# A two-block network kernel on one core: three steps on unsplit weights at the start, another spread of c, and more banks in the convolution stage

## The chip, the cores and the metric

The kernel runs on 1 core of one Trainium2 chip. The metric is device time in microseconds (us); lower is better. Engines are called by the profile's names: PE is TensorE, ACT is ScalarE, DVE is VectorE, POOL is GpSimd, SP is SyncE, whose queue issues all DMAs.

## The reference

Two transformer-like blocks run one after the other on a sequence of 256 tokens with 1024 features, all in float32. What matters here is the beginning of the first block:

```python
c_act = jax.nn.silu(c)
mod = (c_act @ w_ada[i] + b_ada[i]).reshape(bsz, N_MOD, D_MODEL)[:, :, None, :]
shift1, scale1, gate1 = mod[:, 0], mod[:, 1], mod[:, 2]
...
u = rms_norm(x, ln1[i]) * (1.0 + scale1) + shift1
proj = u @ w_in                                   # 1024 -> 13,344 columns
gl, cb, cc, cx, z, xbc, dt = jnp.split(proj, split_at, axis=-1)
...
xbc = jax.nn.silu(causal_depthwise_conv(xbc, ssm_conv_w) + ssm_conv_b)   # 4 taps
dt = jax.nn.softplus(dt + dt_bias)
a = -jnp.exp(a_log)
y = ssd_scan(xs * dt[..., None], dt * a, bs, cs)
```

The rest of both blocks (gates, scan, output projections, an MLP of 4096, two kinds of attention, an MLP of 2816) is large matrix products with the same weights-times-activations form; the change doesn't touch it.

## The kernel before, in words

All activations lie transposed, features on the 128 partitions and 256 tokens along the row. `plan()` cuts all weight matrices into about 141 steps of 1024 rows x 256 columns (1 MB each), `steps[n]`. A step gives two output groups (`nb` 0 and 1) of 128 columns each; group `i = 2*n + nb` is accumulated in one PSUM bank over eight k-tiles.

A product in full precision is made of three products on rounded operands: weights are split into `w_hi` (ACT, `split_hi`, a copy that rounds) and `w_lo` (DVE, `split_lo`, raw minus hi), activations into `uh` and `ul` (`lo_part`, POOL). PE then does hi*hi, hi*lo and lo*hi for each k-tile, 48 matrix products a step (L1160, `product_part`). In steps 4 to 17 (`TAILS`) DVE makes only the first five of eight k-tiles of `w_lo`, and POOL the other three (`split_tail`). The buffers `raw`, `w_hi` and `w_lo` have three slots each.

The first `NAT` = 2 steps are done otherwise: `first_part` multiplies the raw float32 weights by the unrounded activation `uf`, 16 slower products a step, so that nothing has to be split for them. Between these products, `keep_busy` issues idle products so that PE stays active.

The start goes like this. Eight tiles `ada_w` hold the columns of `w_ada` for shift and scale; for each, DVE multiplies it by the activated row c (`cact`, broadcast to all partitions by DMA) and sums along the row, once for scale and once for shift (`early_ada`, L1481), then makes `gain` (L1484). ACT squares x, PE sums the squares over the partitions (`x_sum`), and ACT makes the root (`x_root`, Ln and Exp). POOL multiplies x by the root into `uf`, ACT applies gain and shift twice, for `uh` (rounded) and `uf`, and POOL makes `ul`. PE's `first_part` waits for `uf`.

Steps 0 to 15 are the kind `xbc`, the convolution stage. For group i, ACT initialises `cv` from the bank (L931, the last tap with bias), DVE adds three taps from the bank (L1626, three linked instructions, the last of which frees the bank), and ACT does Silu into `xs` or `bct` (L983). Their banks rotate over `acc0` to `acc2`, and `cv` has two slots.

Woven into the stage are: `dt` (a thin product after step 3, transposed after group 10), its softplus on ACT (`log1p_exp_parts`) and DVE (`softplus`) at `SOFT_AT` = step 5, the cumulative sums at `CUM_AT` = step 8, and from slot 18 (`slot = 2*n + nb`) on sixteen transposes of `xs` (`x_transpose`) in banks M3 and M4 in turn, each of which DVE multiplies by dt into `xdt` (L1648). Transpose i+2 waits until `xdt` i is done. From step 17 on the scan uses M3 and M4 too.

Each engine runs its instructions in the written order; the order on each follows the loops over n and nb. A semaphore wait of one instruction holds all that stands behind it.

## Time and profile before

| | |
|---|---|
| median of 3 runs | 921.14 us (919.28 to 923.37) |
| profiled execution | 923.09 us, of which the span from first to last instruction is 921.1 us |
| PE busy | 891.8 us, 97% of the span |
| DVE busy | 670.0 us, 73% |
| ACT busy | 541.8 us, 59% |
| POOL busy | 316.3 us, 34% |
| mean granted clock of PE | 0.994 |

The share of PE contains idle products of `keep_busy` and products that run slower than later ones, so a high share in the first 45 us doesn't mean that useful work is going at full rate there. What the beginning costs is read from the moment at which the first products on split weights of step 3 can start.

### The profile page before, as it was taken

The numbers are of one execution on the slowest core, as the hardware profiler recorded it, in microseconds if no ns is written. First come the engines' busy times: TensorE is split into PE (matmuls) and PEld (weight loads), VectorE is DVE, ScalarE is ACT, GpSimd is POOL, SyncE is SP. The second block draws the span as 40 slices with busy tenths as digits, with TensorE's granted clock in tenths as the row PEclk, the third lists the DMA queues.
The fourth block names the chain that finished last, engine by engine and source line by source line (L and its number), as shares of the span: only waits on it lengthen the run. The fifth ranks groups of instructions, "written<-read, shape, count | busy, mean of one in ns | idle before, by whom it ended". The sixth has DMA issues, their size and how long they took to land.

```text
span 921.1 us, 17859 instructions
## 1 busy us (share of the span) xinstructions
PE 891.8 (97%) x7390; PEld 859.4 (93%) x7390; DVE 670.0 (73%) x870; ACT 541.8 (59%) x840; POOL 316.3 (34%) x280
## 2 busy tenths in 40 slices
PE   5999999999999999999999999989999999999998
PEld 5899999999999999999999999968888989999998
DVE  5988877887777777868888776678895587755442
ACT  4477556457877864476665444557687674544431
POOL 5623323444377721176655111210003552112100
PEclk9999999999999999999999999998999999999999
DMA  9754555666686678844988878423243449755560
GB/s 365 293 213 179 184 194 219 233 232 251 230 308 241 252 258 311 289 168 141 342 305 288 306 285 284 153 92 138 92 138 122 153 150 335 269 206 174 175 225 24
DMA packets 36112, 203.02 MB, mean 220 GB/s; under 512 B 4928, under 2 KB 6080, under 8 KB 17216
## 3 DMA queue, kind: packets, MB, share of 16 engines
q1 hardware_dynamic: 36032, 201.89, 61.2%
q8 instruction: 58, 0.95, 0.4%
q14 instruction: 22, 0.18, 0.1%
HBM read 200.82 MB, written 1.05 MB: 219 GB/s over the span
## 4 chain that ended last, share of the span: by engine, by line
PE 64%; issue 15%; DVE 10%; ACT 5%; POOL 4%; DMA 1%; SPq 0%; DVEq 0%; ACTq 0%; POOLq 0%
PE acc L1160 56%; ACT w_hi L734 3%; DVE ada_w L1481 2%; POOL rt L622 1%; PE m L1160 1%; POOL ul L628 1%; DMA ada_w<-in_ada_tiles 1%; PE m L1243 1%; PE acc L1123 1%; DVE qk L1727 1%; DVE fr L1447 1%; POOL maps L678 1%; DVE w_lo L1423 1%; DVE rt L1722 1%; DVE maps L1721 1%
## 5 line engine op out<-in xcount | busy, mean ns | idle before, releaser
L1423 DVE TENSOR_TENSOR w_lo<-raw,w_hi 128x2048 fp32r<-128x2048 f32 (+1 forms) x141 | 313.3, 2223 | 129.8 <-ACT w_hi L734 129.6
L1160 PE MATMUL acc<-uh,w_hi 128*128 128x256 f32 x1320 | 374.7, 284 | 4.3 <-POOL ul L628 1.9
L1160 PE MATMUL acc<-ul,w_hi 128*128 128x256 f32 x1320 | 367.5, 278 | 0.0
L1160 PE MATMUL acc<-uh,w_lo 128*128 128x256 f32 x1320 | 367.3, 278 | 0.0
L734 ACT ACTIVATE w_hi<-raw 128x2048 fp32r<-128x2048 f32 x141 | 266.3, 1888 | 77.4 <-PE acc L1160 77.4
L1160 PEld LDWEIGHTS acc<-uh,w_hi 128*128 128x128 f32 x1320 | 250.0, 189 | 11.4 <-issue 4.8
L1160 PEld LDWEIGHTS acc<-ul,w_hi 128*128 128x128 f32 x1320 | 249.9, 189 | 0.4 <-issue 0.2
L1160 PEld LDWEIGHTS acc<-uh,w_lo 128*128 128x128 f32 x1320 | 249.7, 189 | 0.0
L1160 PE MATMUL acc<-hidl,w_hi 128*128 128x256 f32 x432 | 119.2, 276 | 0.0
L1160 PE MATMUL acc<-hidh,w_hi 128*128 128x256 f32 x432 | 119.2, 276 | 0.0
L1160 PE MATMUL acc<-hidh,w_lo 128*128 128x256 f32 x432 | 119.2, 276 | 0.0
L1790 DVE CUSTOM_DVE_ANT_0 colw<-colw,cact,par_all 128x1024 f32<-128x1024 f32 x80 | 117.9, 1480 | 0.0
L628 POOL TENSOR_TENSOR hidl<-fr,hidh 128x256 fp32r<-128x256 f32 x54 | 73.9, 1370 | 115.4 <-ACT hidh L743 115.4
L1160 PEld LDWEIGHTS acc<-hidh,w_hi 128*128 128x128 f32 x432 | 81.1, 188 | 0.0
L1160 PEld LDWEIGHTS acc<-hidl,w_hi 128*128 128x128 f32 x432 | 81.1, 188 | 0.0
L1160 PEld LDWEIGHTS acc<-hidh,w_lo 128*128 128x128 f32 x432 | 81.1, 188 | 0.0
L1626 DVE SCALAR_TENSOR_TENSOR cv<-acc,par_all,cv 128x255 f32<-128x255 f32 (+2 forms) x87 | 41.4, 481 | 10.7 <-ACT cv L931 8.5
L663 POOL TENSOR_TENSOR w_lo<-raw,w_hi 128x768 fp32r<-128x768 f32 x14 | 25.9, 1851 | 65.1 <-DVE w_lo L1423 65.1
L628 POOL TENSOR_TENSOR ycl<-fr,ych 128x256 fp32r<-128x256 f32 x16 | 19.2, 1201 | 80.4 <-ACT ych L743 80.4
L743 ACT ACTIVATE hidh<-fr 128x256 fp32r<-128x256 f32 x54 | 22.2, 411 | 34.5 <-DVE fr L1705 27.0
L622 POOL TENSOR_TENSOR rt<-rt,sq 128x256 f32<-128x256 f32 x20 | 23.2, 1175 | 56.0 <-ACT sq L762 56.0
L1160 PE MATMUL acc<-ych,w_hi 128*128 128x256 f32 x128 | 36.0, 281 | 0.9 <-POOL ycl L628 0.9
(369 smaller groups left out, 1602.9 us busy)
## 6 DMA issues: line engine op xcount, KB each, us to landing
raw<-in_tiles SPq DMA_DIRECT2D x137, 1024.0 KB, 5.6
colw<-in_ada_cols SPq DMA_DIRECT2D x80, 512.0 KB, 5.5
ada_w<-in_ada_tiles SPq DMA_DIRECT2D x8, 1024.0 KB, 17.1
raw<-in_rest SPq DMA_DIRECT2D x4, 768.0 KB, 5.0
cact<-in_c_rows SPq DMA_DIRECT2D x2, 512.0 KB, 4.3
xT<-in_x SPq DMA_DIRECT2D x1, 1024.0 KB, 7.3
first_w<-in_tiles SPq DMA_DIRECT2D x1, 1024.0 KB, 17.1
out<-xT SPq DMA_DIRECT2D x8, 128.0 KB, 4.0
```

Source lines behind the costliest of these rows:

```text
L622: pool.tensor_tensor(rt[:, x, :], first, sq[:, k % 4, :], ALU.add).then_inc(S("sq_added"), 1)
L628: pool.tensor_tensor(lo, uf[:, i, :] if i < YC else fr[:, i % NF, :], hi.bitcast(F32), ALU.subtract).then_inc(S("act_lo"), 1)
L663: pool.tensor_tensor(lo, raw_of(n)[:, TAIL_KT:KB, :], hi.bitcast(F32), ALU.subtract).then_inc(S("lo_tail"), 1)
L678: pool.tensor_tensor(EXS[q % 4], EXS[q % 4], sc[:, q // 4 % 2, :], ALU.mult).then_inc(S("mul_done"), 1)
L734: act.activation(w_hi[:, n % NHL, 0:s.kts, 0:s.cols], raw_of(n), ACT.Copy)\
L743: act.activation(hi, x, ACT.Copy).then_inc(S("act_hi"), 1)
L1123: ins = pe.matmul(out_, raw_of(n)[:, i, nb * P:(nb + 1) * P], uf[:, i, :], start=(i == 0), stop=(i == KB - 1))
L1160: ins = pe.matmul(o, l, r, start=(s.k == 0 and i == 0 and not j), stop=(s.last and i == s.kts - 1 and j == 2))
L1423: dve.tensor_tensor(lo, raw_, hi.bitcast(F32), ALU.subtract).then_inc(S("lo_ready"), 1)
L1481: dve.tensor_tensor_reduce(w, w, cact[:, :], 1.0, ada_b[:, c:c + 1], ALU.mult, ALU.add, mod[:, c:c + 1]).then_inc(S("ada_sum"), 1)
L1626: ins = dve.scalar_tensor_tensor(cv[:, i % 2, o:T], ps[:, 0:T - o], ssm_w[:, 32 * tap + fb:32 * tap + fb + 1], cv[:, i % 2, o:T], ALU.mult ...
L1790: dve.tensor_tensor_reduce(w, w, cact[:, :], 1.0, ada_b[:, c:c + 1], ALU.mult, ALU.add, mod[:, c:c + 1]).then_inc(S("col_sum"), 1)
```

## The change

Five things change, most of them in the first 100 us.

1. `NAT` is 3: steps 0, 1 and 2 are done on unsplit weights. Step 1 is loaded into `colw`, which is otherwise used later, step 2 into a slot of `raw`. The list `HEAD` writes out the order of the 24 pairs (step, k-tile), each of two products, so that a k-tile is used for step 0 and 1 as it arrives and for step 2 somewhat later; `HEAD_BUSY` says how many idle products follow which pair.
2. Only one row of c (4 KB) is loaded. ACT activates it, PE spreads it by two products of a column of ones with half the row each (128x512) into M2 and M3, and ACT copies both to `cact`.
3. DVE scales x by gain and root itself in `early_ada`, into `fr`; ACT only adds the shift, first for `uf` (which `first_part` now waits for) and then for `uh`. POOL keeps only `ul`. The order of the DMAs is new: a small part of the parameters, the first ada tile, x in two halves, the other parameters, and then ada tiles and weights of steps mixed.
4. In the convolution stage all eight banks are used (`CONV_BANKS`), and the convolution has four buffers, two `cv` and two `fr` (`conv_buf`).
5. `dt` goes after step 4 instead of 3 and is transposed after step 7's first group, `SOFT_AT` is 8 instead of 5, DVE's part of softplus comes one step after ACT's, in which ACT now makes 1 + exp itself; `CUM_AT` is 12, the transposes of `xs` begin at slot 21. The splits of weights stand in other places: `split_hi` of step n+4 after the second group of steps 0 to 4, and of step n+2 from step 7 on.

```diff
-NAT = 2
+NAT = 3
+HEAD = ((0, 0), (0, 1), (1, 0), (1, 1), (0, 2), (1, 2), (0, 3), (1, 3), (2, 0), (2, 1), (0, 4), (1, 4), (2, 2),
+        (2, 3), (2, 4), (0, 5), (1, 5), (2, 5), (0, 6), (1, 6), (2, 6), (0, 7), (1, 7), (2, 7))
+HEAD_BUSY = {0: 8, 1: 3, 5: 6, 7: 2}
+CONV_BANKS = ["acc0", "acc1", "acc2", "M0", "M1", "M2", "M3", "M4", "acc0", "acc1", "acc2", "M1", "M2", "M3", "M4", "acc0"] +\
+    (4 * ["acc1", "acc2", "M1", "M2", "acc0"])[0:16]
...
-    SOFT_AT = X0 + 5
-    CUM_AT = SOFT_AT + 3
+    DT_AT = X0 + 4
+    SOFT_AT = DT_AT + 4
+    CUM_AT = X0 + 12
+    XT_SLOT = 21
+    N_EARLY = 5
...
-    stream = [("ada", 0), ("ada", 1), ("ada", 2), ("ada", 3), ("step", 0), ("ada", 4), ("ada", 5), ("step", 1),
-              ("ada", 6), ("ada", 7), ("step", 2), ("step", 3), ("dt", 0)]
+    stream = [("ada", 0), ("x", 0), ("x", 1), ("par", 0), ("step", 0), ("ada", 1), ("ada", 2), ("step", 1), ("ada", 3),
+              ("ada", 4), ("step", 2), ("ada", 5), ("ada", 6), ("ada", 7), ("step", 3), ("step", 4), ("dt", 0)]
...
+            return cv[:, i % 2, :] if i % 4 < 2 else fr[:, i % 2, :]
...
-            pool.wait_ge(S("xroot"), 1)
-            pool.wait_ge(S("ada_sum"), NB)
             for b in range(KB):
-                pool.tensor_tensor(uf[:, b, :], xT[:, b, :], rt[:, 0, :], ALU.mult).then_inc(S("f_ready"), 1)
-                if b:
-                    lo_part(U1 + b - 1)
-            lo_part(U1 + KB - 1)
+                lo_part(U1 + b)
...
-                act.activation(w[:, 1, :], w[:, 0, :], ACT.Exp, scale=-1.0).then_inc(S("sp_e"), 1)
+                if k == 0:
+                    log_exp_table()
+                link(act.activation(w[:, 1, :], w[:, 0, :], ACT.Exp, scale=-1.0))
+                act.activation(w[:, 2, :], w[:, 1, :], ACT.Identity, bias=ones[:, 0:1]).then_inc(S("sp_w"), 1)
...
-            act.activation(cact[:, :], cact[:, :], ACT.Silu).then_inc(S("cact"), 1)
+            act.activation(cact[0:1, :], cact[0:1, :], ACT.Silu).then_inc(S("c_silu"), 1)
             log_exp_table()
+            for half, bank in enumerate((M2, M3)):
+                act.wait_ge(S("c_spread"), half + 1)
+                ins = act.activation(cact[:, half * D // 2:(half + 1) * D // 2], bank[:, :], ACT.Copy)
+            ins.then_inc(S("cact"), 1)
...
                 if b == KB - 1:
-                    split_hi(2)
+                    split_hi(NAT)
                 act.wait_ge(S("f_ready"), U1 + b + 1)
-                act.wait_ge(S("gain0"), b + 1)
-                act.wait_ge(S("ada_sum"), NB * (b + 1))
                 hi, _ = dest(U1 + b)
-                act.activation(hi, uf[:, b, :], ACT.Identity, bias=SH[0][:, b:b + 1], scale=gain[:, 0, b:b + 1])
-                act.activation(uf[:, b, :], uf[:, b, :], ACT.Identity, bias=SH[0][:, b:b + 1], scale=gain[:, 0, b:b + 1])\
-                   .then_inc(S("act_hi"), 1)
+                act.activation(uf[:, b, :], fr[:, b % NF, :], ACT.Identity, bias=SH[0][:, b:b + 1]).then_inc(S("uf_ready"), 1)
+                act.activation(hi, fr[:, b % NF, :], ACT.Identity, bias=SH[0][:, b:b + 1]).then_inc(S("act_hi"), 1)
...
+                if n == 0:
+                    dve.wait_ge(S("xroot"), 1)
+                if n >= NF:
+                    dve.wait_ge(S("act_hi"), n - NF + 1)
+                dve.wait_ge(S("gain0"), n + 1)
+                dve.scalar_tensor_tensor(fr[:, n % NF, :], xT[:, n, :], gain[:, 0, n:n + 1], rt[:, 0, :], ALU.mult, ALU.mult)\
+                   .then_inc(S("f_ready"), 1)
...
-                        if nb == 0 and n != 2:
-                            split_lo(n + 3 if n < 2 else n + 2)
-                        if nb == 1 and n == 5:
+                        if nb == 1 and n < N_EARLY:
+                            split_lo(n + 4)
+                        if nb == 0 and n >= N_EARLY + 2:
+                            split_lo(n + 2)
+                        if nb == 0 and n == SOFT_AT:
+                            signs()
...
-                if n == SOFT_AT:
+                if n == SOFT_AT + 1:
                     softplus(dtr[:, 1:6, :], dtr[:, 0, :], 0, 1.0)
```

The first place at which the order of an engine's instructions matters is DVE's beginning. Before, each ada tile is two row sums (each with the read of its sum) and the gain:

```order
L1497 COPY dsk<-par_all 64x16 x2
L1481 ISA ada_w,mod<-ada_w,cact,par_all 128x1024
L1481 ISA mod 128x1
L1481 ISA ada_w,mod<-ada_w,cact,par_all 128x1024
L1481 ISA mod 128x1
L1484 SCALAR_TENSOR_TENSOR gain<-mod,par_all 128x1
```

In the changed kernel DVE's beginning reads so, from its first row sum on (the parameter work of L1522 to L1531 now stands between the first and the second tile):

```order
L1506 ISA mod 128x1
L1509 SCALAR_TENSOR_TENSOR gain<-mod,par_all 128x1
L1516 SCALAR_TENSOR_TENSOR fr<-xT,gain,rt 128x256
L1522 TENSOR_TENSOR par_all<-par_all 128x64
L1523 TENSOR_TENSOR par_all<-par_all 128x64
L1524 TENSOR_REDUCE small<-par_all 128x1
```

What moved: every tile has one instruction more on DVE, the scaling `fr`, and the first of these, which needs the root of x, stands ahead of the eight small parameter instructions and of the other seven tiles.

The second place is DVE in the convolution stage, around the softplus. Before, the softplus follows at once on `dt`'s bias (L1640), behind the second group of step 5:

```order
L1626 SCALAR_TENSOR_TENSOR cv<-acc,par_all,cv 128x253
L1640 TENSOR_TENSOR cct<-m,par_all 128x64
L1463 TENSOR_SCALAR cct<-cct 128x64
L1464 TENSOR_SCALAR cct<-cct 128x64
L1466 TENSOR_TENSOR cct<-cct 128x64
```

Now, on DVE again, the stretch from the bias of `dt` (L1676, in step 8) over step 9's two groups, the softplus (L1490 to L1789) and step 10's two groups to the first `xdt` (L1684):

```order
L1676 TENSOR_TENSOR cct<-m,par_all 128x64
L1663 SCALAR_TENSOR_TENSOR cv<-acc,par_all,cv 128x255
...
L1450 TENSOR_TENSOR w_lo<-raw,w_hi 128x1280
L1663 SCALAR_TENSOR_TENSOR fr<-m,par_all,fr 128x255
...
L1490 TENSOR_SCALAR cct<-cct 128x64
L1491 TENSOR_TENSOR cct<-cct 128x64
...
L1789 TENSOR_TENSOR dta<-dt_sb,nega 128x64 x2
...
L1684 TENSOR_TENSOR xdt<-m,dt_sb 128x2x128
```

What moved: the softplus stands four steps later, and between its end and the first `xdt` there are only step 10's two groups and the split of step 12.

The third place is ACT at the same point. This is its part of softplus in the changed kernel, between the Silu of group 16 and the start of group 18:

```order
L1011 ACTIVATE xs<-cv 128x256
L842 ACTIVATE cct<-cct 128x64
L790 ACT_TABLE_LOAD
L845 ACTIVATE cct<-cct 128x64
L846 ACTIVATE cct<-cct,ones 128x64
L848 ACTIVATE cct<-cct 128x64
L757 ACTIVATE w_hi<-raw 128x2048
L959 ACTIVATE fr<-m,par_all 128x256
```

What moved: before, ACT loads a table twice in this chain (ahead of L820 and of L822) and waits for DVE in between; now it loads one and has one instruction more, L846.

## Rows read from the trace of the kernel before

**Rows 1.** Busy time of the engines, from the page.

```profile
PE 891.8 (97%) x7390; PEld 859.4 (93%) x7390; DVE 670.0 (73%) x870; ACT 541.8 (59%) x840; POOL 316.3 (34%) x280
```

**Rows 2.** Stretches: us, busy PE, PEld, DVE, ACT, POOL, granted clock, DMA share, GB/s.

```profile
9.60:13.00 3.40, 3.40 (x8) 2.77 (x9) 1.36 (x3) 2.01 (x6) 0.00 (x0) 1.00 1.02 429
13.00:15.00 2.00, 2.00 (x10) 1.70 (x10) 2.00 (x4) 0.43 (x2) 0.00 (x0) 1.00 0.99 418
20.00:30.00 10.00, 10.00 (x48) 8.81 (x47) 10.00 (x14) 2.78 (x6) 8.73 (x7) 1.00 1.02 424
```

**Rows 3.** Chain that ended last, 0 to 140 us: start us, us, what.

```profile
14.21 1.19 DVE ada_w L1481
...
17.22 1.76 DVE ada_w L1481
...
33.02 0.50 ACT uf L844
...
35.12 0.43 PE m L1123 x2
...
48.78 5.44 PE acc L1160 x48
```

**Rows 4.** DVE in order of time, 6 to 42 us.

```profile
6.56 0.22 DVE L1488 TENSOR_TENSOR par_all<-par_all 128x64 f32<-128x64 f32 x1 [6.56 <-DMA par_all<-in_params]
...
7.89 0.37 DVE L1497 COPY dsk<-par_all 64x16 f32<-64x16 f32 x2
...
14.05 0.16 DVE L1484 SCALAR_TENSOR_TENSOR gain<-mod,par_all 128x1 f32<-128x1 f32 x1
...
38.71 0.68 DVE L1484 SCALAR_TENSOR_TENSOR gain<-mod,par_all 128x1 f32<-128x1 f32 x1
```

**Rows 5.** POOL in order of time, 21 to 24 us.

```profile
21.20 0.72 POOL L628 TENSOR_TENSOR ul<-uf,uh 128x256 fp32r<-128x256 f32 x1
21.89 1.72 POOL L654 TENSOR_TENSOR uf<-xT,rt 128x256 f32<-128x256 f32 x1
```

**Rows 6.** ACT in order of time: the start, and the softplus at 72 to 75 us.

```profile
6.56 1.06 ACT L828 ACTIVATE cact<-cact 128x1024 f32<-128x1024 f32 x1 [4.25 <-DMA par_all<-in_params]
...
9.04 1.33 ACT L762 ACTIVATE sq<-xT 128x256 f32<-128x256 f32 x4
...
15.69 0.42 ACT L772 ACTIVATE rt<-rt 128x256 f32<-128x256 f32 x1
...
73.23 1.28 ACT L822 ACT_TABLE_LOAD   x1
74.52 0.26 ACT L822 ACTIVATE cct<-cct 128x64 f32<-128x64 f32 x1
```

**Rows 7.** DVE's x_norm scaling: durations min/median/max in ns, first and last start.

```profile
L1447 DVE SCALAR_TENSOR_TENSOR fr<-xT,gain,mx x24: 468/481/966, 416.4 to 747.8; 128x256 f32<-128x256 f32 x24
```

**Rows 8.** PE in order of time, 73 to 80 us, without most products of L1160.

```profile
78.64 0.38 PE L1160 MATMUL acc<-uh,w_hi 128*128 128x256 f32 x1 [1.47 <-DVE cv L1626]
```

**Rows 9.** Groups by shape, 75 to 180 us: count, busy us, mean ns, idle before.

```profile
L734 ACT ACTIVATE w_hi<-raw 128x2048 fp32r<-128x2048 f32 x17 | 32.5, 1911 | 0.0
...
L1423 DVE TENSOR_TENSOR w_lo<-raw,w_hi 128x1280 fp32r<-128x1280 f32 x10 | 14.8, 1482 | 0.0
L931 ACT ACTIVATE cv<-acc,par_all 128x256 f32<-128x256 f32 x20 | 11.2, 562 | 18.7 <-PE acc L1160 18.5
...
L983 ACT ACTIVATE xs<-cv 128x256 f32<-128x256 f32 x16 | 6.5, 408 | 0.3 <-DVE cv L1626 0.3
```

**Rows 10.** DVE in order of time, convolution stage and the end of softplus.

```profile
75.86 0.36 DVE L1753 TENSOR_TENSOR dta<-dt_sb,nega 128x64 f32<-128x64 f32 x2
...
119.60 1.51 DVE L1626 SCALAR_TENSOR_TENSOR cv<-acc,par_all,cv 128x255 f32<-128x255 f32 x3
121.03 0.41 DVE L1648 TENSOR_TENSOR xdt<-m,dt_sb 128x256 f32<-128x256 f32 x1
...
149.44 0.74 DVE L1670 TENSOR_TENSOR fr<-acc,cv 128x256 f32<-128x256 f32 x2
```

More of the change, by code:

```diff
@@ L134, in plan @@
         s.banks = []
+        if s.kind == "xbc":
+            s.banks = CONV_BANKS[NB * n:NB * n + NB]
+            turn = 2
+            continue
         for nb in range(NB):
@@ L535, in _ @@
                         sp.wait_ge(S("col_sum"), n - 1)
+                    else:
+                        sp.wait_ge(S("acc_ready"), steps[1].g + NB)
                     sp.dma_start(colw[:, n % 2, :], a["ada_cols"][n]).then_inc(S(f"col_in{n % 2}"), 16)
@@ L750, in x_square @@
                 if n == 0:
[L751 removed]
+                    act.wait_ge(S(f"x_in{b // (KB // 2)}"), 16)
                 else:
@@ L891, in _ @@
                 s = steps[n]
-                if 3 <= n < NS - 2 and not split_late(n) and n not in LATE:
+                if N_EARLY + 2 <= n < NS - 2 and not split_late(n) and n not in LATE:
                     split_hi(n + 2)
@@ L982, in _ @@
                         act.wait_ge(S("conv_done"), i + 1)
-                        act.activation(dst, cv[:, i % 2, :], ACT.Silu).then_inc(S("silu_done"), 1)
+                        act.activation(dst, conv_buf(i), ACT.Silu).then_inc(S("silu_done"), 1)
                     if takes and pending:
@@ L1103, in x_sum, with keep_busy @@
                     free["M3"] = ("xroot", ROOT[n])
-            def keep_busy(count):
+            def keep_busy(count, to=M1[:, 0:T]):
                 for _ in range(count):
-                    pe.matmul(M1[:, 0:T], ones[:, :], tri[:, :], start=True, stop=True)
+                    pe.matmul(to, ones[:, :], tri[:, :], start=True, stop=True)
+            pe.wait_ge(S("c_silu"), 1)
+            for half, bank in enumerate((M2, M3)):
+                pe.matmul(bank[:, :], ones[0:1, :], cact[0:1, half * D // 2:(half + 1) * D // 2], start=True, stop=True)\
+                  .then_inc(S("c_spread"), 1)
+            free["M2"] = free["M3"] = ("cact", 1)
             x_sum(0)
             pe.wait_ge(S("pc"), N_CONST)
-            keep_busy(16)
+            take("M3")
+            keep_busy(6, M3[:, 0:T])
             def first_part(n, nb, i):
```

128 lines of the change are left out of this document (64 added, 64 removed).

## The prediction

> **What bounds the kernel now.** The page first: PE is busy for 891.8 us of the span of 921.1 [rows 1], so behind the beginning there is almost nothing to gain but PE's own work and its few idle spots. I therefore read the beginning in the chain of waits, then each engine in order of time.
>
> In the chain the first 33 us hang on DVE. Its row sum of half an ada tile takes 1.19 us from start to next start when it is undisturbed, and 1.76 when it isn't [rows 3]. The disturbance is visible on POOL: an `ul` at 21.20 takes 0.72, and the `uf` that starts right behind it takes 1.72 [rows 5], because it now waits for the row sum and then makes the next one wait. Each POOL instruction that falls into DVE's row sums thus costs DVE about 0.55 us (1.76 - 1.20). From 14.05 to the last gain at 38.71 + 0.61 [rows 4] DVE has seven tiles at 2.47 us, which is 17.3, and thirteen POOL instructions (8 `uf` less the first two, and 7 `ul`) at 0.55, which is 7.2: together 24.5 of 25.3 us. Transfers run at 424 GB/s with a DMA share of 1.02 meanwhile [rows 2], so DMA is close behind.
>
> ACT then makes `uf` in 0.50 [rows 3], PE does the last unsplit products and step 2, and the 48 products of step 3 start at 48.6 (the chain enters them at 48.78) and take 5.44 [rows 3]. This start is the mark by which I measure the beginning: the reader should see that 48.6 us pass before three steps are done.
>
> The second cost is in the convolution stage: PE stood idle for 1.47 us until 78.64, released by DVE's `cv` [rows 8], because softplus had held ACT and DVE and three banks don't cover that.
>
> **The start, step by step.** The activation of c takes 1.06 at 6.56 now, after a wait for the parameters [rows 6]. With a row of 4 KB it should be there near 3 us and activated near 4.1. Then come PE's two products of 128x512: twice the columns of a square sum each. Between 9.60 and 13.00 PE starts 8 instructions in 3.4 us, between 13.00 and 15.00 10 in 2.0, although the granted clock is given as 1.00 in both [rows 2]; the spacing of 0.43 against 0.21 is that of the levels of 1.2 and 2.4 GHz, the slow one after PE had done nothing. At the slow level each spread takes 1.7 us, so M3 is full at 7.6, and with ACT's copies `cact` is ready at 8.4. x, whose halves now stand behind one ada tile, lands at about 8 and 9.3 by the bytes ahead of it. The squares start at 8.5 instead of 9.04 [rows 6].
>
> From the first square to the root's end 7.07 us pass now (9.04 to 16.11) [rows 6]. That is the upper bound: 15.6. If PE runs fast from the start, eight sums at 0.43 give 13.4. PE will have worked for about 3.5 us on the spread just before, as long as it worked slowly before it sped up in the rows; I take 14.0. The Trainium skill (TensorE: Matmul & The Clock Gate, "What's actually happening") says that the clock rises after sustained work and falls in idleness; by it the root would be near 13.5, and the sum would be 0.5 lower. No row here shows what the short pause between spread and sums does.
>
> Now DVE. The first scaling ends at 14.5 (0.48, by the same instruction in x_norm [rows 7]), the parameter work takes 1.70 (6.56 to 8.26) [rows 4], so the second tile starts at 16.2. Per tile: two row sums 2 x 1.20, the gain with its self-wait 0.16 [rows 3, 4], the scaling 0.48: 3.04. POOL issues one `ul` per tile and not two instructions: + 0.55, is 3.59. Seven tiles: 25.1, so the last `fr` is there at 41.3. The bounds of a tile are 3.04 (POOL never in the way) and 4.6 (two disturbed sums and a disturbed gain, 2 x 1.76 + 0.61 [rows 3, 4], with the scaling). The last ada tile has 0.5 MB more ahead of it than before (1.2 us at 424 GB/s); it lands near 35.5, and so isn't last at 3.59.
>
> ACT's `uf` of the last tile is there 0.65 later, at 42.0, since it now comes ahead of `uh`. `split_hi` of step 3, queued ahead of it, waits for weights that land at about 38 and ends at 40.5. PE then has six unsplit products at 0.43 [rows 3] left, 2.6 us: all others fit in before. Step 3 starts at 44.6 instead of 48.6: **-4.0**. The extra PE work of step 2 unsplit (16 x 0.43 = 6.9 against 5.44) is hidden in what was idle products; without that cover it would cost 1.5. `w_lo` of step 3 ends at 41.3 + 2.2 + 0.55 = 44.1, half a microsecond before its use.
>
> **The convolution stage.** The stall of before goes, with 1.47 [rows 8]: **-1.5**. But six groups are finished at once at 44.6, and nothing of steps 4 and up is split. I stepped the four queues forward with spacings from the rows: `w_hi` 1.82, `cv` 0.46, Silu 0.33, `w_lo` of five k-tiles 1.40 (durations less 0.08 to 0.1 of overlap) [rows 9], three taps 1.43 (119.60 to 121.03) [rows 10]; 0.06 for a wait; PE 5.52 a step with its gaps [rows 3]. The same on the kernel before gives a stall of 1.7 where the trace has 1.47.
>
> While they catch up, ACT and DVE wait for each other in a ring, `w_hi`, `w_lo`, three taps, Silu: 1.82 + 1.40 + 1.43 + 0.33 + waits = 5.1 a step. From `w_hi` of step 4 at 46 that gives `w_hi` of step 8 at 66.3, of step 9 at 74.3, and DVE's bias of dt in step 8 at 84.8, while PE ends step 8 at 80.7. From there one chain leads on: ACT's Abs, table, Exp, 1 + exp, Ln 2.4; `w_hi` 11 1.82; `cv` 18 0.46: 89.5. DVE: taps 1.43, `w_lo` 11 1.40 (92.4; PE wants it at 91.9: stall 0.5, and 0.2 for POOL's tail), taps 1.43, softplus 2.66 (76.22 less 73.24, one instruction and a wait less) [rows 6, 10], taps, `w_lo` 12, taps 4.26, `xdt` 0.36: 101.1. PE ends step 11 at 98.4 and has transpose 2 there, which waits for `xdt` 0, and with it all products behind: stall 2.8. Together 3.4; less the 0.3 by which the stepping is too long in the kernel before: **+3.0**. Bounds: 0 (DVE arrives 2.8 earlier, an error of 0.1 in each of 30 links) and 5 (the small sign instructions, moved to step 8, or softplus, caught by POOL's tail of 1.85).
>
> Ln's and Exp's table load is 1.28, and the instruction behind it starts 0.01 later [rows 6]. The Trainium skill (ScalarE: Activation LUTs, "What ACT_TABLE_LOAD costs") gives a drain of some 1.38 us on top of the load. By it the chain through softplus would be 1.4 longer and the new stall 4.4, the result 920.3; the trace shows no drain, so I keep 1.28.
>
> Slots 34 to 36 now hold the last three transposes beside the scan. DVE's `xdt` 15 comes behind `w_lo` 20 and the first `fr` at 149.44 [rows 10], PE wants M4 at about the same time: bounds 0 and 1, I take **+0.3**. The cumulative sums in M0, the four convolution buffers, POOL's `dt_lo` and the later parameter load cost nothing: they lie beside products of PE, and each would cost its own length (at most 2 us) without them. The three transposes moved past step 15 only change place.
>
> **Sum.** -4.0 - 1.5 + 3.0 + 0.3 = -2.2. The profiled execution took 923.09, so 920.9 for one like it; against the median of 921.14, which lies 1.95 below it, **918.9**.
>
> **The rivals.** *No new stall*: DVE and ACT have caught up by step 11, because banks and buffers let them run closer than a ring. For it speaks that all eight banks are used and that ACT's softplus has one table load less; against it that the ring contains no bank. -5.2: 915.9.
>
> *The pace per tile is POOL's*, as before: `ul` still meets two row sums of each tile, the scaling is held too, and a tile takes 4.6. Seven tiles: +7.1, step 3 starts at 51.7, the result is 926.0, slower. For it speaks that such tiles of 4.1 without the scaling exist before, against it that POOL has half as many instructions. It decides from 3.59 + 2.2/7 = 3.9 a tile on.
>
> *The transfers bind the start*: POOL costs DVE nothing, the last `fr` is there 3.04 behind the landing, at 38.6, but `w_hi` 3 holds `uf` until 41.1 and `w_lo` 3 PE until 43.5. Then -5.1 instead of -4.0: 917.8.
>
> **How the numbers follow.** Chances: my forecast 0.52, no new stall 0.30, transfers 0.10, POOL's pace 0.08. The forecast's own range is 917 to 922 (root 13.4 to 15.6, stall 2 to 5). The whole range is 915.0 to 923.0. Half a per cent, 4.6 us, is about what a measurement of this kernel tells from no change; faster by more needs under 916.5: most of "no new stall" and little else, 0.30. Slower by more needs 925.8, at the end of POOL's pace: 0.06. Same: 0.64.
>
> **What would show it.** In the changed profile: the root's Exp ending near 14, the last scaling near 41.3 with tiles 3.6 apart, the first product on split weights near 44.6; DVE's bias of dt near 85; PE idle for 2 to 3 us near 100 with an `xdt` or transpose named. Wrong would be: tiles of 4 us and more, products of step 3 waiting for `w_lo`, or no idle PE before 110.

## The result and the profile after

The changed kernel takes 923.4 us in the median of 20 runs (922.7 to 926.7), the kernel before 921.2 us in 20 runs between them (919.1 to 923.4): ratio 1.0028, 95% interval 1.0020 to 1.0036. It is slower by 2.2 us; 918.9 was predicted, and the time lies above the range. The two profiled executions hardly differ, 923.33 us now (span 921.6) and 923.09 before. That is because the one of before was among its slower runs: its mean granted clock was 0.994, the new one's 0.996. Where its clock fell is shown below.

Busy time, from the page of the changed kernel, against [rows 1]:

```profile
PE 892.8 (97%) x7366; PEld 858.3 (93%) x7366; DVE 666.8 (72%) x874; ACT 538.0 (58%) x842; POOL 305.9 (33%) x273
```

**The start.** ACT in order of time, against [rows 6]:

```profile
8.82 1.34 ACT L785 ACTIVATE sq<-xT 128x256 f32<-128x256 f32 x4 [0.94 <-DMA xT<-in_x]
...
15.19 0.42 ACT L795 ACTIVATE rt<-rt 128x256 f32<-128x256 f32 x1
```

PE between them:

```profile
9.29 5.36 PE L1114 MATMUL m<-sq,ones 128*128 128x256 f32 x16 [2.04 <-ACT sq L785]
```

DVE in order of time, against [rows 4]:

```profile
15.64 0.48 DVE L1516 SCALAR_TENSOR_TENSOR fr<-xT,gain,rt 128x256 f32<-128x256 f32 x1 [4.99 <-ACT rt L795]
...
18.21 1.28 DVE L1506 CUSTOM_DVE_ANT_0 ada_w<-ada_w,cact,par_all 128x1024 f32<-128x1024 f32 x1
...
32.22 1.29 DVE L1506 CUSTOM_DVE_ANT_0 ada_w<-ada_w,cact,par_all 128x1024 f32<-128x1024 f32 x1 [0.44 <-DMA ada_w<-in_ada_tiles]
...
42.47 0.49 DVE L1516 SCALAR_TENSOR_TENSOR fr<-xT,gain,rt 128x256 f32<-128x256 f32 x1
```

The root ends at 15.61, no earlier than the bound that the prediction took from the old duration. The second tile starts at 18.21 and the last `fr` ends at 42.96: 24.75 us for seven tiles, 3.54 each (3.59 was predicted), with one wait of 0.44 us for a transfer in it.

The chain of waits, against [rows 3]:

```profile
27.78 2.59 PE m L1136 x12
...
45.48 1.29 PE m L1157 x6
46.77 5.46 PE m L1194 x48
```

Step 3 enters the chain at 46.77 instead of 48.78. In this pair of profiles the start gained 2.0 us. That is the favourable end: in the profiles of xt23 and log18 below, which have the same start, the 16 instructions of the sums took 6.70 us instead of 5.36, and step 3 enters the chain at 48.31 and 48.10.

**The convolution stage.** DVE in order of time; before it, the one POOL instruction beside it:

```profile
85.88 1.84 POOL L686 TENSOR_TENSOR w_lo<-raw,w_hi 128x768 fp32r<-128x768 f32 x1 [2.42 <-DVE w_lo L1450]
```

```profile
86.09 1.67 DVE L1543 TENSOR_SCALAR nega<-nega 128x32 f32<-128x32 f32 x1
87.79 0.23 DVE L1676 TENSOR_TENSOR cct<-m,par_all 128x64 f32<-128x64 f32 x1
...
92.84 1.51 DVE L1663 SCALAR_TENSOR_TENSOR fr<-m,par_all,fr 128x255 f32<-128x255 f32 x3 [3.40 <-ACT fr L959]
...
97.10 0.65 DVE L1490 TENSOR_SCALAR cct<-cct 128x64 f32<-128x64 f32 x1
...
104.40 0.42 DVE L1684 TENSOR_TENSOR xdt<-m,dt_sb 128x256 f32<-128x256 f32 x1
```

The reader is to see three things: the sign of `nega`, 32 numbers a row, takes 1.67 us and ends with POOL's tail; DVE then stands idle for 3.40 us; `xdt` 0 is ready at 104.82. ACT in order of time says what DVE waits for in between:

```profile
88.05 0.26 ACT L842 ACTIVATE cct<-cct 128x64 f32<-128x64 f32 x1 [3.20 <-DVE cct L1676]
88.33 1.28 ACT L790 ACT_TABLE_LOAD   x1
...
90.46 1.91 ACT L757 ACTIVATE w_hi<-raw 128x2048 fp32r<-128x2048 f32 x1
92.27 0.54 ACT L959 ACTIVATE fr<-m,par_all 128x256 f32<-128x256 f32 x1
```

ACT itself had been idle for 3.20 us, waiting for the bias of dt. PE pays for it twice (PE in order of time, without the products between):

```profile
95.81 0.39 PE L1194 MATMUL acc<-uh,w_hi 128*128 128x256 f32 x1 [2.10 <-DVE w_lo L1450]
...
104.96 0.66 PE L1284 MATMUL m<-ident,xs 128*128 128x128 f32 x2 [2.85 <-ACT xs L1011]
```

The second wait is put down to ACT's `xs`, which ended at 104.83; transpose 2 writes the bank that `xdt` 0 reads, and that ended at 104.82. Behind it the clock is at its lower level for three microseconds (stretches; the columns are those of [rows 2]):

```profile
105.00:106.00 1.00, 1.00 (x5) 1.00 (x6) 0.93 (x3) 0.38 (x1) 0.00 (x0) 0.50 0.19 25
106.00:107.00 1.00, 1.00 (x7) 1.00 (x6) 1.00 (x2) 0.73 (x2) 0.00 (x0) 0.50 0.51 139
107.00:108.00 1.00, 1.00 (x7) 1.00 (x7) 1.00 (x3) 1.00 (x1) 0.29 (x1) 0.50 0.88 360
108.00:109.00 1.00, 1.00 (x9) 1.00 (x9) 0.93 (x3) 0.49 (x1) 1.00 (x1) 0.90 1.02 434
```

The 24 products behind the transposes take 4.01 us in the chain instead of 2.75: 1.3 us. Together: -2.0 (start), -1.5 (old stall), +5.0 (two waits), +1.3 (clock) are +2.8. At the second group of scores, in slot 38, the changed kernel is 2.3 us behind the kernel before (155.75 against 153.47), and the medians differ by 2.2. ACT's split of step 23 shows the same 2.29 us (kernel before, then changed):

```profile
165.37 1.92 ACT L734 ACTIVATE w_hi<-raw 128x2048 fp32r<-128x2048 f32 x1
167.66 1.92 ACT L757 ACTIVATE w_hi<-raw 128x2048 fp32r<-128x2048 f32 x1
```

So nothing behind the convolution stage is needed to explain the result. That the two numbers are this close is partly luck, since this profile has an early root and a full fall of the clock. In the medians the clock's part is mostly smaller: the mean granted clock is 0.9962 over the 20 runs of the changed kernel, and 0.9964 to 0.9969 over four sets of runs of the kernel before and 0.9977 over a fifth. As an estimate, that is 0.2 to 0.7 us, and 1.4 against the fifth.

Behind step 23 the two profiles part and meet again. The distance is 3.03 us at the split of step 95 (614.89 against 611.86) and 0.46 at that of step 103 (683.14 against 682.68). It grows in one step of 0.7 us near 400 us, which six of the 18 profiles show, one with the old start among them. What closes it is a fall of the clock in the kernel before, in a part that the change doesn't touch. Two stretches of the kernel before, then one of the changed kernel:

```profile
642.00:645.00 3.00, 3.00 (x11) 2.25 (x12) 2.90 (x6) 1.97 (x2) 0.00 (x0) 0.50 0.16 66
645.00:648.00 3.00, 3.00 (x17) 3.00 (x15) 2.87 (x4) 0.00 (x0) 0.00 (x0) 0.50 0.00 0
```

```profile
645.00:648.00 3.00, 3.00 (x23) 2.65 (x24) 2.90 (x6) 1.77 (x2) 0.00 (x0) 1.00 0.13 55
```

PE has waits of 1.6 to 2.5 us there in every kernel of this document. Over all 18 profiles, its clock was at the lower level for between 0 and 10 us from 600 to 660 us, and the way from the split of step 95 to that of step 103 took 66.7 to 70.9 us. This is as much as the runs of one kernel differ by (919.1 to 923.4 before).

### The profile page after: what moved, and what is told of

Read it like the earlier page. It is cut to its first block, busy times and chain, and to the rows that moved or that the text cites. A ratio compares the mean times of both kernels' runs of the same rounds, so it can differ in the third digit from the quotient of the medians.

```text
span 921.6 us, 17809 instructions
## 1 busy us (share of the span) xinstructions
PE 892.8 (97%) x7366; PEld 858.3 (93%) x7366; DVE 666.8 (72%) x874; ACT 538.0 (58%) x842; POOL 305.9 (33%) x273
## 4 chain that ended last, share of the span: by engine, by line
PE 61%; issue 15%; DVE 12%; ACT 6%; POOL 4%; DMA 1%; SPq 0%; ACTq 0%; DVEq 0%; POOLq 0%
PE acc L1194 50%; ACT w_hi L757 3%; PE m L1194 2%; DVE w_lo L1450 2%; POOL rt L647 1%; PE m L1157 1%; DVE fr L1663 1%; PE acc L1157 1%; POOL ul L653 1%; PE m L1270 1%; DVE qk L1763 1%; DMA xT<-in_x 1%; DVE cv L1663 1%; DVE fr L1474 1%; POOL maps L701 1%
## 5 line engine op out<-in xcount | busy, mean ns | idle before, releaser
L1194 PE MATMUL acc<-uh,w_hi 128*128 128x256 f32 x1224 | 346.0, 283 | 4.7 <-DVE w_lo L1450 2.1
L1194 PE MATMUL acc<-ul,w_hi 128*128 128x256 f32 x1224 | 340.0, 278 | 0.0
L1194 PE MATMUL acc<-uh,w_lo 128*128 128x256 f32 x1224 | 339.9, 278 | 0.0
L1194 PEld LDWEIGHTS acc<-uh,w_hi 128*128 128x128 f32 x1224 | 230.8, 189 | 11.4 <-issue 4.5
L1194 PEld LDWEIGHTS acc<-ul,w_hi 128*128 128x128 f32 x1224 | 230.8, 189 | 0.4 <-issue 0.2
L1194 PEld LDWEIGHTS acc<-uh,w_lo 128*128 128x128 f32 x1224 | 230.9, 189 | 0.0
L1723 DVE SCALAR_TENSOR_TENSOR xT<-acc,mod,xT 128x256 f32<-128x256 f32 x31 | 14.4, 480 | 29.7 <-PE acc L1194 29.5
```

What stands on the lines that cost most here:

```text
L1194: ins = pe.matmul(o, l, r, start=(s.k == 0 and i == 0 and not j), stop=(s.last and i == s.kts - 1 and j == 2))
L1723: dve.scalar_tensor_tensor(xT[:, b, :], ps, GATE[gate][:, b:b + 1], xT[:, b, :], ALU.mult, ALU.add).then_inc(S("x_ready"), 1)
```

## Experiments

Two theories went in. **A**: the start's gain is lost in the convolution stage, where the softplus chain is too late for `xdt` 0. **B**: that chain isn't on the path; the start's own work (six blocks unsplit, scaling on VectorE) costs the time. The table has the results. A run's mean granted clock varied between 0.989 and 1.000, and in the kernel before, between 0.994 and 1.000, that alone is worth 4 us (on one chip, 923.6 us at 0.994 and 919.1 at 1.000). The column "at clock 0.998" therefore compares only the runs at 0.998 with those of the kernel before at 0.998 on the same chip and in the same set of runs, in brackets how many there were. It leaves out what a stall costs by bringing the clock down, and on one chip the runs of the kernel before at 0.998 differ by 0.6 us between two sets. The last column is from the one profile of each kernel: where ACT's split of step 23 starts, against the 165.37 us of the kernel before. It is free of the spread from 600 to 660 us, but not of that of the root and of the clock in the convolution stage.

| kernel | median us | ratio to before (95%) | at clock 0.998 | step 23 in the profile |
|---|---|---|---|---|
| changed kernel | 923.4 | 1.0028 (1.0020 to 1.0036) | | +2.29 |
| signs_early | 922.5 | 1.0006 (0.9989 to 1.0022) | +0.1 (3) | +2.73 |
| xt23 | 921.0 | 0.9990 (0.9975 to 1.0005) | -0.3 (7) | +0.87 |
| fill_m0 | 925.3 | 1.0032 (1.0017 to 1.0048) | +3.3 (5) | +3.38 |
| before_banks | 920.2 | 0.9990 (0.9973 to 1.0007) | -1.0 (5) | -0.61 |
| fill5 | 921.1, one run | | | +1.25 |
| signs_xt23 | 919.5 | 0.9970 (0.9954 to 0.9985) | -1.8 (1) | -0.99 |
| warm | 924.1 | 1.0023 (1.0008 to 1.0037) | +1.3 (2) | +0.52 |
| all3 | 919.5 | 0.9981 (0.9965 to 0.9998) | -2.1 (4) | -2.11 |
| dt3 | 922.9 | 1.0012 (0.9992 to 1.0032) | +1.3 (1) | +1.44 |
| log18 | 919.0 | 0.9972 (0.9952 to 0.9993) | -1.5 (4) | +0.35 |
| signs_log18 | 916.4 | 0.9949 (0.9928 to 0.9970) | -3.6 (2) | -3.07 |
| signs_log_xt22 | 919.9 | 0.9983 (0.9968 to 0.9999) | -1.5 (2) | -0.96 |
| sl_warm | 917.6 | 0.9956 (0.9937 to 0.9975) | -4.9 (3) | -3.98 |
| sl_twobuf | 916.8 | 0.9947 (0.9928 to 0.9967) | -4.4 (3) | -3.62 |
| before_banks_log | 918.6 | 0.9969 (0.9954 to 0.9984) | -3.2 (5) | -2.30 |
| sl_lean | 916.4 | 0.9958 (0.9940 to 0.9977) | -4.1 (1) | -4.55 |

### signs_early

```diff
             split_lo(NAT)
+            signs()
...
                         if nb == 0 and n == SOFT_AT:
-                            signs()
                             dve.wait_ge(S("dt_tr"), 1)
```

> The changed kernel with one edit: the five small operations of signs() run on VectorE right behind the first w_lo at the start, not in slot 16 ahead of the dt bias. Theory A (the gain of the start is lost in the convolution stage, where the softplus chain ends at xdt 0 at 104.82 us while TensorE waits for it from 101.94): the sign of nega takes about 0.18 us again instead of 1.67, the dt bias starts near 86.3 instead of 87.79, xdt 0 and with it TensorE's wait are 1.5 us earlier, the granted clock may stay at 1.00 behind the shorter wait: 1.5 to 2.5 us less than the changed kernel's 923.4, about 921.4. Rival B (the chain is not on the path; the start's products and VectorE's scaling cost the time): 923.4, no change. Rival C (another operation on VectorE is caught by GpSimd's copy instead): the chain's end moves by under 0.5 us, 923.

DVE in order of time at the start, and then a stretch:

```profile
46.52 0.18 DVE L1543 TENSOR_SCALAR nega<-nega 128x32 f32<-128x32 f32 x1
```

```profile
105.00:110.00 5.00, 5.00 (x26) 5.00 (x25) 3.85 (x7) 2.24 (x3) 1.83 (x1) 0.50 0.74 231
```

The sign takes 0.18 where POOL is idle, the wait for `w_lo` 11 is gone, and the ratio falls from 1.0028 to 1.0006, 2.0 us of 1.5 to 2.5 expected. That speaks for A and against B; the two intervals still touch, so this run alone doesn't settle it. In this profile the wait for `xdt` 0 stays (2.85 us), since PE without its first wait comes to it sooner, and the clock stays at 0.50 for over 5 us; with a root 1.1 us later (first `fr` at 16.70), this is why its step 23 is no earlier than the changed kernel's.

### xt23 and dt3

```diff
-    XT_SLOT = 21
+    XT_SLOT = 23
```

> The changed kernel with XT_SLOT 23 instead of 21: the transposes of x and the xdt products stand two slots later, in slots 23 to 38. Theory A: TensorE's idle time of 2.85 us before transpose 2 is gone, because it reaches it 5.5 us of products later, and the 1.26 us that the products behind it lost at granted clock 0.50 are gone too; the 2.10 us before step 11 stay, and the shared slots 34 to 38 cost 0.3 to 1.0 more: 923.4 - 4.1 + 0.7 = 920.0 us. Rival B (chain not on the path): 923.4 or above. Rival D (the waits in slots 34 to 38, where transposes, scores and y products share M3 and M4, give it back): 922.5 to 924.

PE in order of time, and the stretch behind:

```profile
97.33 0.48 PE L1194 MATMUL acc<-uh,w_hi 128*128 128x256 f32 x1 [2.31 <-DVE w_lo L1450]
```

```profile
98.00:101.00 3.00, 3.00 (x17) 3.00 (x16) 2.76 (x9) 1.83 (x4) 1.19 (x1) 0.52 0.22 38
```

One wait is gone, the other stays, and now the clock falls behind that one. The time is 0.38% lower, 3.5 us of 4.1 expected without the slots' price.

```diff
-    DT_AT = X0 + 4
+    DT_AT = X0 + 3
```

> The changed kernel with DT_AT = X0 + 3 instead of X0 + 4: dt's products, transposes, bias and softplus stand one step (two slots, 5.5 us) earlier, while the transposes stay in slots 21 to 36. Theory A (the softplus chain ends too late for the transposes): xdt 0 is no longer waited for (2.85 us gone) and the clock stays at 1.00 (1.3 to 3.3 us gone); the wait for a w_lo that the chain puts off moves one step earlier and stays near 2 us: ratio to the kernel before 0.999 to 1.000, as with XT_SLOT 23 alone. Rival C (not the chain's place but ScalarE's and VectorE's work as a whole is too much in these steps, so that a wait of the same size comes up elsewhere): ratio 1.002 or above.

PE's waits from 46 to 200 us (in total, times, longest):

```profile
PE acc L1194 <- DVE w_lo L1450: 1.8, 1, 1.8
PE m L1395 <- DVE fr L1663: 1.5, 1, 1.5
```

`xdt` 0 is no longer waited for. But the same 3.40 us of idle DVE stand one step earlier, `w_lo` is late there, dt's own products now come before their bank is free (1.5), and the clock is 0.51 from 93 to 96 us. The ratio of 1.0012 lies between the two theories' numbers, and its interval holds both. What the profile shows is that moving the chain as a whole doesn't remove the stall: the chain carries it with it.

### fill_m0 and fill5

```diff
+                    if slot == 23:
+                        take("M0")
+                        keep_busy(11, M0[:, 0:T])
                     if XT_SLOT <= slot < XT_SLOT + 16:
```

> The changed kernel with 11 idle products (ones by tri into M0, 0.23 us each at full clock, 2.5 us together) on TensorE in slot 23, ahead of transpose 2, where it waits for 2.85 us anyway. The wait for xdt 0 stays as it is. Theory A with the clock as a part of the loss: the products behind the wait run at granted clock 1.00 and not at 0.50 from 105 to 108.2 us: 1.3 us less, 922.1 us. Rival E (the clock falls whatever stands there, or the step at 105 us waits for VectorE's ring anyway and the lost 1.26 us lie beside other waits): 923.4 us, no change.

PE in order of time:

```profile
102.68 4.91 PE L1136 MATMUL m<-tri,ones 128*128 128x256 f32 x22
107.43 0.38 PE L1284 MATMUL m<-ident,xs 128*128 128x128 f32 x2
```

My expectation had the idle product at half its cost. The eleven ended 1.9 us behind `xdt` 0 (105.56), and the time rose. The granted clock was 1.00 from 102 to 110 us. Five of them:

> The changed kernel with 5 idle products into M0 in slot 23, ahead of transpose 2. With 11 of them each took 0.446 us (22 instructions in 4.91 us), not the 0.23 that was expected, so that they ended at 107.43 us, 1.9 us behind xdt 0, and gave back what the clock had won; five take 2.2 us and end before xdt 0 does. Theory A: granted clock 1.00 behind the wait, and transpose 4 comes 4.5 us behind transpose 2 (as with 11 idle products) instead of 6.0 us, with transpose 2 right behind xdt 0. Rival E: the clock falls all the same, and the distance stays at 6.0 us.

```profile
105.30 0.41 PE L1284 MATMUL m<-ident,xs 128*128 128x128 f32 x2 [0.69 <-ACT xs L1011]
109.76 0.44 PE L1284 MATMUL m<-ident,xs 128*128 128x128 f32 x2
```

From transpose 2 to 4 it is 4.5 us, 6.0 in the changed kernel (104.96 to 110.94). The wait itself keeps its end. With work in it the clock stayed up, in both profiles. That this is owed to the work isn't shown: in the profile of warm the clock stayed up as well, behind a wait of 2.92 us with nothing in it.

### signs_xt23, log18, signs_log18 and signs_log_xt22

> The changed kernel with both edits that were tried alone: signs() at the start and XT_SLOT 23. Theory A: with signs() at the start no wait for w_lo was left (0 instead of 2.1 us), and with XT_SLOT 23 no wait for xdt 0 (0 instead of 2.85 us), so that TensorE is never idle between 47 and 139 us: 923.4 - 5.0 - 1.3 + 0.5 (shared slots) = 917.6 us by the sum, or about 2.5 us under what XT_SLOT 23 gives alone (its ratio to the kernel before was 0.999). Rival G (a third wait comes up behind the two, for instance for the sums of the decay in slot 24): the ratio stays at 0.999.

PE's idle time fell to 1.4 us, in two waits for `w_lo`, and the ratio to 0.9970: 1.8 us under xt23, of some 2.5 expected. The waits that are left, 0.40 us for `w_lo` 11 and 0.99 for the next one, are a small form of rival G. The next edit goes to the order on ACT:

```diff
+                    if n == SOFT_AT + 1 and nb == 0:
+                        log1p_exp_parts(dtr[:, 1:6, :], dtr[:, 0, :], 0)
-                if n == SOFT_AT:
-                    log1p_exp_parts(dtr[:, 1:6, :], dtr[:, 0, :], 0)
```

> The changed kernel with ScalarE's part of the softplus (Abs, table load, Exp, Identity, Ln) behind the Silu of slot 18 instead of at the end of step 8, ahead of w_hi 11 and of the bias of slot 18. Theory A in its finer form: VectorE stood idle for 3.40 us before the taps of slot 18, because ScalarE first waited for the dt bias (3.20 us) and then did two table loads' and w_hi 11's worth of work; with the order turned, that idle time is gone, xdt 0 is over 2 to 3 us earlier, the wait for w_lo 11 is under 0.5 us and the one for xdt 0 under 1 us, and the clock stays up: 3 to 5 us less than the changed kernel, 919 to 920 us, ratio 0.998 to 0.999. Rival: the softplus on VectorE then waits for Ln instead, the stall keeps 2 us or more, ratio 1.001 or above.

> log18 with signs() at the start as well, XT_SLOT 21. Theory A: another 1.5 us off the chain; TensorE's idle time from 47 to 139 us is under 0.5 us, without the later transposes' price in slots 34 to 38: 0.5 to 1.5 us under the version with signs() at the start and XT_SLOT 23 (its ratio was 0.997), 917.5 us, ratio 0.996. Rival: 0.997 or above, because what the chain no longer takes is waited for at the sums of the decay or in the scan.

ACT in order of time in signs_log18, for the rows of 88.05 to 92.27 above:

```profile
86.36 1.91 ACT L757 ACTIVATE w_hi<-raw 128x2048 fp32r<-128x2048 f32 x1
88.17 0.55 ACT L959 ACTIVATE fr<-m,par_all 128x256 f32<-128x256 f32 x1
...
89.32 0.24 ACT L842 ACTIVATE cct<-cct 128x64 f32<-128x64 f32 x1
89.58 1.28 ACT L790 ACT_TABLE_LOAD   x1
```

and DVE:

```profile
92.29 1.51 DVE L1665 SCALAR_TENSOR_TENSOR fr<-m,par_all,fr 128x255 f32<-128x255 f32 x3 [0.50 <-ACT fr L959]
93.72 0.18 DVE L1490 TENSOR_SCALAR cct<-cct 128x64 f32<-128x64 f32 x1
...
100.56 0.42 DVE L1685 TENSOR_TENSOR xdt<-m,dt_sb 128x256 f32<-128x256 f32 x1
```

`w_hi` 11 and the bias of slot 18 come before Abs and the table load instead of behind them. DVE's idle time falls from 3.40 to 0.50, `xdt` 0 is there at 100.98, and PE's longest wait in the stage is 0.24 us, the clock 1.00. log18 alone took 5.2 us off the changed kernel (0.9972 against 1.0028, some 3 to 7 us by the two intervals; 3 to 5 expected), with a wait of 2.1 us before transpose 2 left (under 1 was expected). This difference is clear of both intervals, and it is the firmest evidence for A. With signs() early it is 0.9949, better than both kernels.

> signs_log18 with XT_SLOT 22. If xdt 0 is still waited for there by up to 1 us with XT_SLOT 21, one slot more (2.75 us) takes that away, for 0.2 us in the slots shared with the scan: 0 to 0.8 us less than signs_log18. If the chain is early enough already: 0.2 us more, within what is measured.

PE's waits in it:

```profile
PE m L1250 <- DVE xdt L1685: 1.8, 1, 1.8
PE m L1270 <- DVE xdt L1685: 0.5, 1, 0.5
```

That one missed. With XT_SLOT 22 slot 34 holds transpose 12, in M3, where the first scores (L1250) go too, and slot 37 holds transpose 15, in M4, where the first y products (L1270) go; both wait for an `xdt`, 2.3 us, ten times what I had put for the shared slots. With 21 and 23 these slots hold no transpose or one in the other bank of the two, and no such wait was seen.

### before_banks, before_banks_log and sl_twobuf

> The kernel before with one part of the change: CONV_BANKS and the four buffers of conv_buf (cv and fr) in the convolution stage; start, dt chain and slots as before. Theory A: the wait of 1.47 us before the products of 78.64 us is gone, and nothing takes its place: 921.2 - 1.5 = 919.7 us. Rival F (the ring of ScalarE and VectorE sets the pace, so more banks only let TensorE wait later in the stage): 921.2 us, no change.

```diff
+CONV_BANKS = ["acc0", "acc1", "acc2", "M0", "M1", "M2", "M3", "M4", ...
...
-                        if i >= 2:
-                            act.wait_ge(S("silu_done"), i - 1)
-                        act.activation(cv[:, i % 2, :], ps, ...
+                        if i >= 4:
+                            act.wait_ge(S("silu_done"), i - 3)
+                        act.activation(conv_buf(i), ps, ...
```

PE's waits from 46 to 200 us:

```profile
PE m L1265 <- DVE cum_t L1756: 0.8, 1, 0.8
PE acc L1168 <- DVE w_lo L1431: 0.6, 1, 0.6
```

The old wait of 1.47 [rows 8] is gone, and two others sum to 1.4. What the banks are worth by themselves is between nothing and 1 us (0.6 in the profile at step 23), and isn't settled by these runs.

> The kernel before with CONV_BANKS, the four buffers, and the cure: ScalarE's part of the softplus in the form of the changed kernel (1 + exp on ScalarE, its own table load), behind the Silu of slot 12 instead of at the end of step 5, VectorE's part at the end of step 6. The start is that of before, signs() stand at the start anyway. If the start of the change is worth its 2.0 us of the profile: this one stays 2 us above signs_log18, near 919 us, ratio 0.997. If the start is worth nothing and all came from the cure: 917, ratio 0.995. If before has nothing to cure (its waits of 0.6 and 0.8 us stay): 920.2, ratio 0.999.

Here ACT's part of the softplus stands behind the Silu of slot 12, in the changed kernel's form, and DVE's at the end of step 6. PE waits for nothing from 46 to 200 us but 0.2 us for POOL, and the ratio is 0.9969, as the first reading said. signs_log18 has the same cure, the changed start, and 0.9949. The ratios differ by 1.8 us with intervals that overlap, the differences at clock 0.998 by 0.5, and step 23 by 0.8. So the start is worth 0.5 to 2 us. The profiles say what this depends on: where the sums of squares take 6.7 us with either start (6.71 here, 6.70 in xt23), step 3 enters the chain at 49.17 here and at 48.31 there, 0.9 us apart. In the pair of the section on the start it was 2.0. The softplus in its new form and place is worth about 2 us in the kernel before too (0.9990 to 0.9969, again with intervals that overlap, and 1.7 at step 23); form and place weren't tried apart.

```diff
-            return cv[:, i % 2, :] if i % 4 < 2 else fr[:, i % 2, :]
+            return cv[:, i % 2, :]
...
-                        if i >= 4:
-                            act.wait_ge(S("silu_done"), i - 3)
+                        if i >= 2:
+                            act.wait_ge(S("silu_done"), i - 1)
```

> signs_log18 with the two buffers of cv alone in the convolution stage (conv_buf gives cv only, ScalarE's bias waits for the Silu of two blocks before); CONV_BANKS stay. If the four buffers are worth what the prediction's term for the old stall says (1.5 us): 918.5, ratio 0.9965. If ScalarE's order (bias 20 behind Silu 18 and so on) never needs more than two: no difference, 0.995.

No difference: once nothing holds up the ring, the four buffers are worth nothing that these runs can tell (their intervals are 2 us to each side).

### warm, all3, sl_warm and sl_lean

```diff
+            def warm(count):
+                for _ in range(count):
+                    pe.matmul(M1[:, 0:P], ones[:, :], ones[:, :], start=True, stop=True)
+            warm(4)
             pe.wait_ge(S("c_silu"), 1)
...
             free["M2"] = free["M3"] = ("cact", 1)
+            warm(4)
             x_sum(0)
```

> The changed kernel with 4 idle products (ones by ones, 128 columns) on TensorE ahead of the spread of c and 4 behind it, where it stood idle (up to 3.50 us, and from 7.25 to 9.29 us). Theory H (the sums of squares ran slow because TensorE came to them cold): the 16 instructions take 3.6 us (0.223 each) instead of 5.36 to 6.70, the root is there near 13.9 us instead of 15.6 to 17.2 us. Of what that is worth two readings: H1, the last fr, step 3 and the end come 1.7 us earlier; H2, the ada tiles land too late for it (VectorE waited 0.44 us for tile 5 at 32.22 us), so that the start gains at most 0.5 us against the profile of the changed kernel. The time then is eaten by the stall behind the softplus chain only in part, since that chain moves too: H1 921.7, H2 923.0 us. Rival: the clock of the sums stays low, 923.4.

DVE in order of time:

```profile
14.99 0.49 DVE L1523 SCALAR_TENSOR_TENSOR fr<-xT,gain,rt 128x256 f32<-128x256 f32 x1 [3.68 <-ACT rt L795]
...
32.40 1.55 DVE L1513 CUSTOM_DVE_ANT_0 ada_w<-ada_w,cact,par_all 128x1024 f32<-128x1024 f32 x1 [1.27 <-DMA ada_w<-in_ada_tiles]
```

The 16 instructions of the sums take 4.28 us (5.28 to 6.73 in the profiles with this start and without these products), and the first `fr` comes at 14.99. But DVE waits until 32.40 for tile 5, and the last `uh` starts at 43.40, in the changed kernel at 43.41. H2 holds: tile 5 isn't there earlier. In a kernel whose root is late (17.2) there is no such wait, and the last `uh` starts at 44.3; the early root takes that away and no more. The time was 924.1, above the 923.0 of H2, with an interval that overlaps that of the changed kernel.

> The changed kernel with the three edits together: signs() at the start, XT_SLOT 23, and the idle products around the spread of c. Theory A: no idle time of TensorE over 0.3 us between 47 and 140 us, step 3 as early as in warm: 0.5 to 1.7 us under signs_xt23, some 4 to 6 us under the changed kernel and 2 to 4 under the kernel before, ratio 0.996 to 0.998. Rival B (the stage's end is set by something else, for instance VectorE's ring of 5.2 us per step against TensorE's 5.5): the same as signs_xt23.

Both readings of all3 asked for a time at or under signs_xt23's; the ratios are 0.9981 and 0.9970, with intervals that overlap. The times show no gain by the warm start there; in the profiles step 23 is 1.1 us earlier.

> signs_log18 with the 8 idle products around the spread of c. In the run with these alone the sums of squares took 4.28 us instead of 5.4 to 6.7 and the first fr stood at 14.99 us instead of 15.6 to 17.2, but VectorE then waited 1.27 us for ada tile 5. Theory H2 (behind the root the transfers of the ada tiles set the start): step 3 starts 0.4 us earlier than in the profile of the changed kernel, and the time is that of signs_log18 or up to 1 us less (ratio 0.994 to 0.995). Theory H1 (the root sets the start, as the prediction's sum had it): 1.7 us or more less, ratio 0.993 or under. Rival: the 0.7 us by which the idle products put off the copies of c cost it, ratio 0.9955 or above.

> signs_log18 with HEAD_BUSY = {0: 8, 1: 3}: the six and the two idle products behind HEAD's places 5 and 7 are left out, 16 instructions or 3.45 us of TensorE's work between 27.8 and 33.0 us. If these are why TensorE is behind ScalarE's last uf, the 48 products of step 3 start 2.6 to 2.7 us behind the last uf's end instead of 3.3, 0.6 us earlier: ratio 0.994 to 0.995. Rival: TensorE then stands idle between tiles, the granted clock falls, and the products of the last tiles run slow: later than now, ratio 0.996 or above.

sl_warm's ratio of 0.9956 is above both theories and at the rival's number, with an interval that holds H2 as well; at clock 0.998 it is 0.6 us under signs_log18, and at step 23 0.9. So it says no more than that an early root brings under 1 us. H1 asked for 0.993 or under, which is outside the interval. In sl_lean (the idle products behind places 5 and 7 of HEAD left out) step 3 starts at 45.39, 2.55 us behind the last `uf`; in signs_log18 it starts at 47.80, 3.45 behind it. The idle products did stand in the way, by 0.9 us (0.6 were expected), and the rest of the distance is the root, whose first `fr` is at 15.57 here and at 17.01 there. The ratio of 0.9958 doesn't show it.

## Why the prediction was wrong

Three terms of the sum failed: the start, put at -4.0, measured -2.0 at its best; the new stall, put at +3.0, measured +5.0; and the clock behind the stall, which had no term, measured +1.3 in the profile. The root and the stall both came out at the upper bounds that the prediction had given them.

*What bounds it*: right. What separates the two kernels lies in the start and the convolution stage; the spread of each by itself lies mostly behind, from 600 to 660 us.

*The root at 14.0*: wrong, it ended at 15.61, the upper bound. The step that failed is "PE will have worked for about 3.5 us on the spread just before". PE worked for 3.75 us on it, stood idle for 2.04, and the sums ran mostly at the low level. With products before and in that pause (warm) they took 4.28 us. The Trainium skill (TensorE: Matmul & The Clock Gate, "What's actually happening") has the clock rise with sustained work and fall in idleness. The trace agrees in the direction; the root near 13.5 that I worked out by it didn't come, since I gave the pause no price. Even with the pause filled the sums took 4.28 us in warm and 4.99 in sl_warm, not eight at 0.43.

*3.59 a tile, w_hi and w_lo of step 3*: right, 3.54. POOL's single `ul` costs one row sum 0.46 us (1.74 against 1.28). The parameter work before the second tile took 2.1 us (16.12 to 18.21), and 1.70 was predicted.

*The transfers*: "it lands near 35.5, and so isn't last" spoke of tile 7 only (the tiles counted from 0). Tile 5 came at 32.2, and with a root at 14.0 DVE would have waited for it. So the 4 us weren't there to be had with this order of transfers: in warm, with the root earlier, the last `uh` came no earlier than in the changed kernel.

*The last unsplit products*: 2.6 us behind `uf` were taken; in the chain it was 3.3 (43.50 to 46.77), because PE works without a pause from 27.78 on, 3.45 us of it on idle products (2.59 in the row above, and 0.86).

These make the start -2.0 instead of -4.0.

*The new stall of +3.0*: the mechanism was right, chain by chain, and was shown by log18 and signs_early. Its size was 5.0. The bias of dt came at 87.79 instead of 84.8. The sign of `nega` is 1.5 of that, which the prediction had in its upper bound and not in its value, although POOL's tail starts right behind the `w_lo` that `signs()` follows; the later step 3 is 2.0, and the stepping was 0.5 too long. The Trainium skill (SBUF — State Buffer, "SBUF: two separate sides") has VectorE and GpSimd share a pair of ports as a lock for a whole instruction; the sign's 1.67 beside POOL and 0.18 without it agree with that.

*The clock*: left out. The prediction counted the stall's length and nothing behind it; 1.3 us in this profile, more in that of signs_early, nothing in that of warm.

*The old stall of -1.5*: removed as named, but by itself (before_banks) it was replaced by 1.4 us of others; the sum kept it as a gain.

*Slots 34 to 36, +0.3*: not measured apart. The neighbour with XT_SLOT 22 pays 2.3 there.

By the sum with measured terms: -2.0 - 1.5 + 5.0 + 1.3, and 0.3 for the slots, are +3.1, with 2.2 to 2.3 measured. The 0.8 between stays open. The terms are those of one profile: in a usual run the start gains less than 2.0, and the clock costs less than 1.3.

## What to carry to other kernels

When a start is made faster, everything behind it that was just in time is late by as much: find the longest chain that doesn't move with it, and price it link by link, each small instruction at its disturbed duration. An engine that waits in program order for a result, ahead of work that others need and that is ready, is the place to look: turning that order brought 5.2 us; moving the chain as a whole (dt3) brought 1.5, which is within the noise. Before comparing two profiles, look where in each the granted clock falls: here that alone makes 4 us between runs of the same kernel, more than the change, and a marker ahead of the falls compares better than the end. Comparing at equal mean clock helps too, but it takes away what a stall costs by the clock.
